# A two-layer hybrid backbone: loads of the up/down seam issued in another order, boundary work moved from GpSimd to VectorE, copies ahead of squares, four landing places for late half units

## The reference, cut to what matters

```python
h = h + mod[2] * rms_norm(o_lat, g[1])
f = channel_mixer(modulate(rms_norm(h, g[2]), mod[3], mod[4]), w_ff1[layer], w_ff2[layer])   # square(relu(a @ w1)) @ w2
h = h + mod[5] * rms_norm(f, g[3])
if want_ctx:   # layer 0 only: the same for hc with mod_c
    ...
```

## Time and profile before

| | |
|---|---|
| median of the runs | 1631.89 us |
| the profiled execution, its time | 1634.09 us |
| its span (first to last instruction) | 1631.6 us |
| what lies around the span | 2.5 us |
| busy: PE, DVE, ACT, GpSimd | 1572.4, 1282.0, 846.7, 188.4 us |

### The profile page before, as it was taken

The page is one execution under the profiler, slowest core; times in us unless marked ns, Lnnn a source line. Parts: engine busy times, 40 slices in busy tenths (PEclk is TensorE's granted clock), DMA queues, the critical chain, the costliest instruction groups (busy, mean ns, idle before and its releaser), DMA issues.

```text
span 1631.6 us, 24960 instructions
## 1 busy us (share of the span) xinstructions
PE 1572.4 (96%) x9392; PEld 1358.8 (83%) x9392; DVE 1282.0 (79%) x2037; ACT 846.7 (52%) x1515; POOL 188.4 (12%) x188
## 2 busy tenths in 40 slices
PE   7999999999999999998999989998999899999997
PEld 5999888878779999987888777987877778888886
DVE  5889787676789788769989587876784777787778
ACT  5433466765475555545444556315675654445442
POOL 1000276332000000000000240003340000000000
PEclk9999999999999999999999999999999999999999
DMA  8533521013325555496853313533023133222221
GB/s 353 188 130 130 139 74 35 11 63 135 149 82 202 181 210 204 180 347 215 302 200 97 129 37 134 205 125 121 2 79 129 52 115 117 104 103 91 104 90 52
DMA packets 55991, 220.96 MB, mean 135 GB/s; under 512 B 6208, under 2 KB 19392, under 8 KB 41024
## 3 DMA queue, kind: packets, MB, share of 16 engines
q1 hardware_dynamic: 55872, 219.37, 38.2%
HBM read 181.33 MB, written 27.26 MB: 128 GB/s over the span
## 4 chain that ended last, share of the span: by engine, by line
PE 52%; DVE 6%; DMA 3%; ACT 3%; issue 2%; SPq 0%; POOL 0%; DVEq 0%; ACTq 0%
PE ps L1834 12%; PE ps L1467 9%; PE ps L1469 8%; PE ps L1468 8%; PE ps L1810 7%; PE ps L1613 2%; PE ps L1640 2%; DMA mod_raw<-in_w_ada_t 1%; PE ps L1591 1%; PE ps L1601 1%; DMA token_rows<-hs 1%; DVE h L3144 1%; DMA raw<-in_w_ff 1%; DMA down_land<-in_w_ff 1%; DVE ada_junk L3402 1%
## 5 line engine op out<-in xcount | busy, mean ns | idle before, releaser
L1467 PE MATMUL ps<-whi,ahi 128*128 128x256 f32 (+1 forms) x496 | 149.7, 302 | 4.2 <-DVE wlo L2987 2.2
L1469 PE MATMUL ps<-whi,alo 128*128 128x256 f32 (+1 forms) x496 | 147.8, 298 | 0.0
L1468 PE MATMUL ps<-wlo,ahi 128*128 128x256 f32 (+1 forms) x496 | 147.7, 298 | 0.0
L1834 PE MATMUL ps<-whi,tok_hi 128*128 128x512 f32 x336 | 133.6, 398 | 9.1 <-DVE tok_lo L3729 7.6
L1469 PE MATMUL ps<-ahi,wlo 128*128 128x512 f32 (+2 forms) x368 | 138.1, 375 | 0.0
L1834 PE MATMUL ps<-whi,tok_lo 128*128 128x512 f32 x336 | 132.1, 393 | 0.0
L1834 PE MATMUL ps<-wlo,tok_hi 128*128 128x512 f32 x336 | 132.1, 393 | 0.0
L1467 PE MATMUL ps<-ahi,whi 128*128 128x512 f32 (+1 forms) x336 | 127.6, 380 | 0.4 <-ACT relu L2776 0.4
L1468 PE MATMUL ps<-alo,whi 128*128 128x512 f32 (+1 forms) x336 | 127.2, 379 | 0.0
L2674 ACT ACTIVATE whi<-down_land 128x1024 fp32r<-128x1024 f32 x56 | 59.3, 1059 | 111.5 <-PE ps L1834 90.7
L3402 DVE SCALAR_TENSOR_TENSOR ada_junk<-mod_raw,silu_rows 128x1024 bf16<-128x1024 f32 x80 | 97.7, 1221 | 20.9 <-DMA mod_raw<-in_w_ada_t 18.4
(11 more groups left out here) (365 smaller groups left out, 4426.6 us busy)
## 6 DMA issues: line engine op xcount, KB each, us to landing
raw<-in_w_ff SPq DMA_DIRECT2D x48, 1024.0 KB, 4.8
tok_in<-token_rows SPq DMA_DIRECT2D x56, 384.0 KB, 3.1
mod_raw<-in_w_ada_t SPq DMA_DIRECT2D x16, 1024.0 KB, 7.9
down_land<-in_w_ff SPq DMA_DIRECT2D x32, 512.0 KB, 6.8
token_rows<-hs SPq DMA_DIRECT2D x40, 384.0 KB, 3.4
raw<-in_w_ada_t SPq DMA_DIRECT2D x12, 1024.0 KB, 4.9
mod_raw<-in_w_ada_t SPq DMA_DIRECT2D x24, 512.0 KB, 4.9
raw<-in_w_in_odd SPq DMA_DIRECT2D x9, 1024.0 KB, 5.1
```

The lines of the kernel that those rows point to most:

```text
L1467: pe.matmul(dst, lhs[0], rhs[0], start=first, stop=False)
L1468: pe.matmul(dst, lhs[0], rhs[1], start=False, stop=False)
L1469: return pe.matmul(dst, lhs[1], rhs[0], start=False, stop=last)
L1834: ins = pe.matmul(dst, x_[m % 4][:, k, a], w_[:, k, :], start=first and not chained and k == 0 and j == 0, stop=last and k == 1 and j == 2 ...
```

## The change

It has five parts. (1) Up phase: one modulation step of a chunk moves from before the add of c11 to the chunk's end, and ACT copies the open sum "u1" before relu and square of c11. (2) Seam: SP asks for tokens 0 and 1 at the head of chunk 7; of the weight blocks it asks for b11 of each chunk first, then in steps 0 to 2 for b22 and b12 of chunks 1 to 3, and in steps 6, 8, 9 and 10 for b21; stores of chunk 7 and two modulation loads come some steps later; ACT splits tokens 0 before weight block 1, DVE makes s4 in step 9. (3) Boundary: what GpSimd did from step 50 on is done by DVE. (4) ACT's split of the weights of unit 4 goes ahead of `context_slices(4..7)`, DVE's into the midst of the context's `alo`. (5) The last twelve half units use four places: 8 and 9, in the scratch `S2`, which are free after the head processing of unit 4, and 5 and 6.

```diff
+        mod_raw += [... for i, where in enumerate((C + 24 * KB, C + 28 * KB, B + 8 * KB, S2, S2 + 4 * KB))]
-        slot_of_half = [5 + k % 3 for k in range(15)] + [5 + (k - 15) % 2 for k in range(15, 24)]
+        slot_of_half = [5 + k % 3 for k in range(12)] + [(8, 9, 5, 6)[k % 4] for k in range(12, 24)]
...  SP, up phase, then the seam
                     else:
                         weight_block(0, "b11")
+                        token_part(0)
+                        token_part(1)
                     for name in ("s3", "s1", "s2"):
                         store(c - 1, name)
...
-                    else:
-                        token_part(0)
-                        token_part(1)
-                for name in ("b12", "b22"):
-                    weight_block(0, name)
-                for name in ("b11", "b12", "b22"):
-                    weight_block(1, name)
+                weight_block(1, "b11")
+                weight_block(0, "b22")
+                weight_block(2, "b11")
                 store(7, "a22")
-                for name in ("b11", "b12", "b22"):
-                    weight_block(2, name)
+                weight_block(0, "b12")
                 token_part(2)
                 token_part(3)
-                for name in ("b11", "b12", "b22"):
-                    weight_block(3, name)
-                for c in range(4):
-                    weight_block(c, "b21")
+                weight_block(3, "b11")
                 for m, (name, c) in enumerate(DOWN_PARTS):
...
-                    if m == 1:
-                        for block_ in ("s3", "s1", "s2", "a12"):
+                    if m < 3:
+                        weight_block(m + 1, "b22")
+                        weight_block(m + 1, "b12")
+                    elif m == 3:
+                        for block_ in ("s3", "s1"):
                             store(7, block_)
-                    elif m in (3, 5):
-                        modulation_unit(MOD_UP + (m - 3) // 2)
-                    elif m == 6:
+                    elif m == 4:
+                        for block_ in ("s2", "a12"):
+                            store(7, block_)
+                    elif m in (5, 7):
+                        modulation_unit(MOD_UP + (m - 5) // 2)
+                    elif m in (6, 8, 9, 10):
+                        weight_block((6, 8, 9, 10).index(m), "b21")
+                    elif m == 11:
                         store(7, "s4")
...  SP, modulation_half
+                elif k in (12, 13):
+                    sp.wait_ge(s_post, POST["in1"] + 3)
                 else:
-                    sp.wait_ge(s_ada, pieces_before(MOD_DOWN) + (k - 2 if k < 17 else k - 1))
+                    sp.wait_ge(s_ada, pieces_before(MOD_DOWN) + k - (2 if k < 12 else 4 if k in (14, 15) else 3))
...  ACT, input_projection, ff_in_phases
+                    if layer == 1 and u + 2 < n_units:
+                        split_hi(w0 + u + 2)
                     if (layer, u) == (1, 2):
                         context_slices(range(4, KT))
-                    if layer == 1 and u + 2 < n_units:
-                        split_hi(w0 + u + 2)
...
+                    snapshot(c, "u1")
                     finish("c11", c)
-                    snapshot(c, "u1")
...
                 down_hi(0)
-                down_hi(1)
                 tokens_hi(0)
                 finish("c12", 7)
+                down_hi(1)
                 tokens_hi(1)
...  GpSimd: the loop over steps 50 to 55 and all gates go, with the normalization of tile 2
-            for m in range(TOKENS_BY_POOL, len(DOWN_PARTS)):
...
-            for t in (4, 5):
-                gate_columns(t, 0, D)
...  DVE, input_projection, ff_in_phases
-                        split_groups("pre10", 1)
-                    if layer == 1 and u + 2 < n_units:
+                        split_groups("pre10", 1, lambda k: split_lo(w0 + 4) if k == 5 else None)
+                    elif layer == 1 and u + 2 < n_units:
                         split_lo(w0 + u + 2)
...
                     token_sum_of(c - 1, "s2")
-                    if c > 1:
-                        modulation_step()
                     add_block(c, "c11")
...
                     if c < 7:
                         part_lo("p2", c + 1)
+                    modulation_step()
                     if c == 1:
-                        modulation_step()
                         modulation_step()
...
-                    if m < TOKENS_BY_POOL:
-                        tokens_lo(m)
-                    if m == 4:
+                    tokens_lo(m)
+                    if m == 9:
                         token_sum_of(7, "s4")
...
+                    elif m in (52, 53):
+                        for t in (2 * m - 104, 2 * m - 103):
+                            gate_columns_of("post01", t, 512, 512, 1)
...
-                post_root(post, 0, 3)
+                for t in range(3):
+                    gate_columns_of(post, t, 0, 512, 0)
                 add_sum(13, "c21", "q43", 0)
+                post_root(post, 0, 4)
+                gate_columns_of(post, 3, 0, 512, 0)
                 back(0)
-                for t in range(3):
-                    settled(t)
+                settled()
+                for t in range(4):
                     residual(post, t)
-                post_root(post, 3, 1)
-                settled(3)
-                residual(post, 3)
                 pre_root(pre, 0, 3)
                 pre_root(pre, 3, 1)
                 normalize(pre, 2, 3)
+                normalize(pre, 1, 2)
                 add_sum(13, "c21", "q44", 1)
...
                 norm_entry(pre, W_IN1, ...)
+                wait_groups_before(dve, tg_index["gate01", 1, 1] + 1)
+                for t in (4, 5):
+                    gate_columns_of(post, t, 0, D, 0)
                 post_root(post, 4, 2)
```

More of the change, by code:

```diff
@@ L232, in build @@
                    for i, where in enumerate((A + 12 * KB, A + 20 * KB, B + 8 * KB, A + 30 * KB, H))]
-        mod_raw += [place(f"mod_raw{5 + i}", [P, D], F32, where) for i, where in enumerate((C + 24 * KB, C + 28 * KB, B + 8 * KB))]
+        mod_raw += [place(f"mod_raw{5 + i}", [P, D], F32, where) for i, where in enumerate((C + 24 * KB, C + 28 * KB, B + 8 * KB, S2, S2 + 4 * KB))]
         down_at = (1152, C + 16 * KB, C + 32 * KB, C)
@@ L577, in build @@
         NORM_READY = {"pre00": 0, "pre01": 3, "pre10": 6, "pre11": 9}
-        TOKENS_BY_POOL, GATED_BEFORE = 50, 6
         QUARTERED = {W_OUT0: 0, W_OUT0 + 3: 1, W_FF0: 2, W_FF0 + 1: 3, W_IN1: 4, W_IN1 + 1: 5,
@@ L704, in mod_value @@
             k = 2 * (j - MOD_DOWN) + mt
-            return 16 * ({5: 2, 6: 2, 7: 7}[slot_of_half[k]] + slot_of_half[:k + 1].count(slot_of_half[k]))
+            return 16 * ({5: 2, 6: 2, 7: 7, 8: 3, 9: 2}[slot_of_half[k]] + slot_of_half[:k + 1].count(slot_of_half[k]))
         UP_PARTS, MOD_UP, MOD_DOWN = len(BLOCK_PARTS), 11, 16
@@ L2913, in normalize_first @@
                                        ALU.mult, ALU.mult).then_inc(s_xn, 1)
[L2915 to L2920, removed]
             normalize_first(1, (0, 1))
@@ L2943, in _ @@
                     zero_rows(1)
-            for m in range(TOKENS_BY_POOL, len(DOWN_PARTS)):
[L2945 to L2948, removed]
-                if m == 52:
-                    wait_groups_before(pool, tg_index["gate01", 0, 1] + 1)
-                    for t in range(NTL):
-                        gate_columns(t, 1)
-            for t in range(NTL):
-                gate_columns(t, 0)
-                if t == 3:
-                    pool.wait_ge(s_rstd, NORM_READY["pre10"] + 1)
-                    pool.tensor_scalar(xn[:, 2, :], h[:, 2, :], norm_rstd[:, 10:11], 1.0, ALU.mult, ALU.mult).then_inc(s_xn, 1)
-            wait_groups_before(pool, tg_index["gate01", 1, 1] + 1)
-            for t in (4, 5):
-                gate_columns(t, 0, D)
             for i in range(N_ODD):
@@ L3871, in ff_in_phases @@
                             copy_group(("gate01", 0, half))
+                        wait_groups_before(dve, tg_index["gate01", 0, 1] + 1)
                     elif m == 51:
                         add_sum(11, "c22", "q7")
+                    elif m in (52, 53):
+                        for t in (2 * m - 104, 2 * m - 103):
+                            gate_columns_of("post01", t, 512, 512, 1)
                     elif m == 54:
@@ L3879, in ff_in_phases @@
                 post, pre = "post01", "pre10"
-                assert gated[0] == GATED_BEFORE, gated[0]
-                gated[0] += 10
-                settled = lambda t: dve.wait_ge(s_gated, GATED_BEFORE + 5 + t)
+                settled = lambda: dve.wait_ge(s_gated, gated[0])
                 back = lambda i: dve.wait_ge(s_hback[i], 16)
-                post_root(post, 0, 3)
+                for t in range(3):
+                    gate_columns_of(post, t, 0, 512, 0)
                 add_sum(13, "c21", "q43", 0)
+                post_root(post, 0, 4)
```

(17 more changed lines are left out.)

## The result

Median 1604.39 us (1603.24 to 1604.94, six runs) against 1630.86 for the kernel before in the same session: ratio 0.9839, 95% interval 0.9826 to 0.9853. That is 1.6% faster, within the 2% band. The forecast was 1606, its own range 1602 to 1610. One execution of 2880 us stands among those of the kernel before; it moves their median by less than 0.1 us.

A forecast was written before the change was run, and what follows sets the result against it. The prediction took PE, busy 1572.4 of 1631.6 us, as the bound, so only its waits and slow clock counted. Terms summing to 26.2 us gave 1607.9, less 2.2 for the median: forecast 1606, range 1602 to 1610.

The forecast's parts named there:

- copy and step, up phase: Up phase, chunk 2: PE's wait for ACT's copy goes, 2.6 us plus 1.7 of slow clock, 4.3 gained.
- seam: Up to down, 712 to 765 us: three PE waits of 7.6 us and 3.5 of slow clock go, 11.1 gained.
- GpSimd's work: 1.5 + 3.6 - 3.8: Boundary: 1.5 from GpSimd waits, 3.6 from smaller gap (1.9) and half its clock loss (1.7); 3.8 lost at third input unit.
- split ahead of the context slices: Near 1018 us: PE's wait for wlo goes, 2.2 us plus 1.5 of clock, 3.7 gained (at least 2.2).
- four landing places: Half units, 1070 to 1108 us: PE's wait for first exponentials goes, 3.7 + 0.4 + 1.7 = 5.8 gained.
- D: Rival, chance 0.05: asking step by step starves the seam; each b12 landing L above 9.6 us costs L - 9.6 per chunk.
- starting when PE has finished its first tile: Boundary: DVE's 12.8 us chain to the first transposes starts at 946.7, leaving a gap of 1.7 to 1.8, not 3.7.
- New wait at the third unit: Third input unit, 991 us: two gates delay DVE's lo split; PE waits 2.1 plus 1.7 of clock, 3.8 lost.
- No DVE wait over 1 us: Sign at the landing places: changed kernel's profile shows no DVE wait for mod_raw over 1 us.
- B: Rival, chance 0.18: DVE, not transfers, holds seam and boundary; seam gives 6, boundary nothing, gap may stay 3.7; 1614 us.
- C: Rival, chance 0.12: halves land no faster with four places, so the 5.8 us stay out; 1612 us.
- A: Rival, chance 0.17: no new wait at 991, or clock stays up at the boundary; 2 to 6 us more gained, 1600 to 1604.

The follow-up runs named there:

- E2: Changed kernel with the up phase put back: modulation step before the add of c11, copy of the open sum behind relu and square; 1609.25 us (+4.9).
- E3: Changed kernel with three and then two landing places for the late half units, as before, instead of four; 1609.18 us (+4.8).
- E1: Changed kernel with the whole seam put back: SP's old order of loads and stores, ACT's old order, s4 in step 4; 1616.05 us (+11.7).
- E4: Changed kernel with GpSimd doing the boundary work again (six token splits, ten gates, one normalization); 1606.77 us (+2.4).
- E5: Changed kernel with the split of the gkv unit's weights behind the context slices again, on ACT and DVE; 1606.27 us (+1.9).
- E7: Changed kernel with only ACT's old order at the seam (block 1 split before the tokens of step 0), SP's new order kept; 1603.68 us (-0.7).
- E11: Changed kernel with each of the seam's three b12 blocks asked for one step later; 1606.54 us (+2.2).
- E8: Changed kernel with only SP's old order of loads and stores at the seam (with the sum of s4), ACT's new order kept; 1615.96 us (+11.6).
- E6: Changed kernel with DVE's low split of the third input unit moved ahead of the context tiles' root; 1603.72 us (-0.7).
- E13: The changed kernel run again, nothing altered; 1605.36 us, ratio 0.9851 to the kernel before.
- E12: Changed kernel with third unit's low split ahead of the context tiles' root, ACT's old seam order, one modulation step moved from unit 4 to 5; 1601.65 us.
- E10: Changed kernel with only the modulation step put back before the add of c11, the copy staying ahead of relu and square; 1608.25 us (+3.9).

## Why the prediction was right, and where not

The forecast came within 1.6 us, by terms that mostly held and misses of both signs: the gain was foreseen as 26.2 and is 26.5 in the medians, and 1.0 of the 1.6 is that the kernel before took 1630.86 in the session of the result and not 1631.89. Each term against its undoing (medians; good to 1 us, those of E2 and E3 to 2):

| term | foreseen | measured |
|---|---|---|
| copy and step, up phase | 4.3 | 4.9 (E2) |
| seam | 11.1 | 11.7 (E1) |
| GpSimd's work: 1.5 + 3.6 - 3.8 | 1.3 | 2.4 (E4) |
| split ahead of the context slices | 3.7 | 1.9 (E5) |
| four landing places | 5.8 | 4.8 (E3) |
| sum | 26.2 | 25.7 |
| whole change | 26.2 | 26.5 |

The parts add up to the whole, but that they do so this closely is partly luck. By aligned matmuls of single profiles the stretches of the five terms gave, in the whole change, 5.3, 11.7, 2.2, 4.0 and 5.5 us, and undone one by one 4.7, 10.7, 2.0, 1.3 and 3.8. At the split and the landing places part of the gain came from the rest of the change.

**Up phase.** Right in place and nearly in size. The step that was wrong is "Gain 2.6 + 1.7 = 4.3": the sum left out stalls of 0.2 to 0.7 us in each later chunk, which the list of waits hardly holds, and it charged a fall of the clock that E2's profile doesn't have at its 2.64 us wait. The kernel before has one behind a wait of the same 2.64 us at the same place.

**Seam.** Right that the transfers' order was the cause and that DVE's slack would do. Wrong that ACT's order was part of it (E7). The condition of D was nearer than foreseen: the prediction put the point at which it begins to cost at a landing of 9.6 us and expected some 5; the slowest landing was 10.3. What it costs beyond that was overstated: the price L - 9.6 takes the landing as fixed, and E11 shows that it shrinks when the request comes later (10.3 to 7.5 us for that same block). The Trainium skill (DMA: Bandwidth & Descriptors, "Rules for kernel authors") says to issue a DMA early and wait for it late; by that rule E8's order should be the better, and it is 11.6 us slower. Here early large transfers stood ahead of small urgent ones on one set of engines: a token part landed up to 15.7 us after its request, against 8.8 in order of need.

**Boundary.** Foreseen 1.7 to 1.8, measured 2.34. Timeline of the changed kernel, DVE, ACT and PE, which answers to the earlier trace rows:

```profile
927.42 1.89 DVE L3101 TENSOR_TENSOR xn<-xn,gate 128x512 f32<-128x512 f32 x3
929.22 0.68 DVE L3741 TENSOR_TENSOR xn<-xn,ps 128x512 f32<-128x512 f32 x1
...
932.97 4.88 DVE L3124 SCALAR_TENSOR_TENSOR h<-xn,norm_rstd,h 128x1024 f32<-128x1024 f32 x4
...
940.58 1.42 DVE L3030 TENSOR_SCALAR xn<-h,norm_rstd 128x1024 f32<-128x1024 f32 x2
...
942.05 2.40 PE L1337 MATMUL ps<-kons,xn 128*128 128x128 f32 x20 [2.34 <-DVE xn L3030]
```

The chain from the add of q43 to PE takes 12.8 us (929.22 to 942.05), the number of the prediction to a tenth. The step that failed is "starting when PE has finished its first tile": three gates of 1.89 us stand ahead of the add, with no idle between, and hold it some 0.6 us (PE's last matmul ends at 939.7; by the prediction's 11.1 from the first tile to there, that tile was ready at 928.6; worked out, not seen).

That moving the work to DVE gained anything was argued from one row, DVE's split of 2.83 us. E4 shows a stronger one. Timelines of E4, the root on DVE and the gates on GpSimd:

```profile
929.07 1.22 DVE L3019 TENSOR_SCALAR chy<-chv 128x3 int32<-128x3 int32 x1
930.32 1.20 DVE L3026 TENSOR_TENSOR cha<-chy 128x3 f32<-128x3 f32 x1
931.56 1.21 DVE L3027 TENSOR_TENSOR cha<-cha,chv 128x3 f32<-128x3 f32 x1
```

```profile
928.98 3.78 POOL L2923 TENSOR_TENSOR xn<-xn,gate 128x512 f32<-128x512 f32 x3
```

Three operations on three columns take 1.2 us each while GpSimd runs three gates of 1.26 each, and 0.17 without it (the changed kernel, from 938.17 on). A root of 1.4 us becomes one of 4.7; the rest of its operations, after the gates, take 0.15 to 0.16 again. The Trainium skill (SBUF — State Buffer, "SBUF: two separate sides") calls the port pair that the two engines share an exclusive lock, in which the later one blocks for the whole instruction of the other. The rows agree: each of the three starts just behind the beginning of a gate and ends with it. The Trainium skill names there, on DVE's side, operations in a 2-port mode or with two inputs in SBUF; the first of the three shows one input, and its mode stands in no row.

**New wait at the third unit.** Foreseen 2.1 with 1.7 of clock, measured 1.93 with 1.7; the fall behind it came in 4 of 10 profiles. Timeline of DVE and PE, which answers to the earlier trace rows:

```profile
959.32 2.36 DVE L3101 TENSOR_TENSOR xn<-xn,gate 128x1024 f32<-128x1024 f32 x2
...
968.12 2.28 DVE L2967 TENSOR_TENSOR wlo<-raw,whi 128x2048 fp32r<-128x2048 f32 x1
...
970.46 0.50 PE L1471 MATMUL ps<-ahi,whi 128*128 128x512 f32 x1 [1.93 <-DVE wlo L2967]
```

**Split ahead of the context slices.** The term that was mis-sized most: 1.9 for 3.7. The prediction took the wait of before as it stood; but other parts of the change had already moved both sides of it (E5). The new wait, which makes PE late, is likely one of them; no run shows it by itself.

**Landing places.** Right in mechanism. "No DVE wait over 1 us" was wrong: three of 1.25 to 1.78 are left, hidden from PE; one of them, at unit 4, is what E6 uncovers.

**Rivals.** B is out at the seam and half true at the boundary (2.3, not 3.7). C is out (E3). Of A, the new wait came, but the clock stayed up at the boundary in the profiled execution; by E13 that was luck, worth 0.6 to 0.8 us by aligned matmuls. D did not come: two blocks were late by a quarter of a microsecond, which PE's slack took up, and asking still later cost 2 us and not 10 (E11).

## What to carry to other kernels

When loads share one set of DMA engines, issue them in the order in which they are needed, with the small urgent ones in front, and check the landing of the latest against its slack: here two blocks were 0.2 us late after the change, which cost PE nothing. A wait that goes uncovers the next in its shadow (E6: 1.9 us of wait gone, a new one of 0.8 come), so look one unit further on the engine that was late. Before work is given to GpSimd, look for DVE operations of a few columns in the same stretch: here they grew from 0.17 to 1.2 us each.

## What the runs showed of the hardware

**The same program with the same waits has a fall of the clock or has none.** Behind the boundary's wait of 2.3 us PEclk fell in 9 of the 12 profiles that have it; behind the wait of 1.9 at the third unit, in 4 of 10. Behind 2.64 us in the up phase it fell in the kernel before and not in E2; behind 2.90 in E1 it did not. By (1 - clock) x length a fall comes to 1.7 us; behind waits of 3.4 to 3.7 us it was once that (E4, E1, and the kernel before at 1111) or twice, 3.4 (E8 from 715 to 730, the kernel before at 961). What sets it was not tried.

**A fall does not cost everywhere what (1 - clock) x length says.** By aligned matmuls the one behind the third unit's wait costs 1.6 us, the one at the boundary only 0.6 to 0.8. There PE, after its first transposes, waits 0.5 us for DVE's alo in the three profiles without a fall (the changed kernel's, E8, E12), and the nine with one have no such wait: part of the slow stretch lies over it. So charge such a wait with the chance of a fall times what the stretch behind it can't absorb; the prediction's half at the boundary was the right kind of number, the full 1.7 at the others was not.

**A profile's first 30 us vary too.** In the profiles of E2 and E3 the clock was low until about 26 us (in the changed kernel's it was full), and by 36 us they were 2.1 to 2.2 us behind. The low clock alone doesn't explain it: in E1 and E10 it was low until about 21 us, and they lost nothing by 36. So single profiles differ by some 2 us before anything has been changed, and single profiles were used here for where time goes, medians for what an edit is worth.
